# The first block's norm sums: squares made one pair of tiles at a time, GpSimd adds some of them, and TensorE sums half as many tiles

## The reference

```python
def rmsnorm(x, g):
    xf = x.astype(jnp.float32)
    y = xf * lax.rsqrt(jnp.mean(xf * xf, axis=-1, keepdims=True) + EPS)
    return y.astype(x.dtype) * g

for l in range(DEPTH):                                   # DEPTH = 2
    mod = c_act @ w_ada[l] + b_ada[l]                    # shift, scale, gate, twice
    hdn = modulate(rmsnorm(x, norm1_g[l]), shift1, scale1)        # norm 1: 1024 features
    proj = hdn @ w_in[l]
    q = to_heads(rmsnorm(q_lat, q_norm_g[l]) @ w_uq[l], ...)      # q latents: 768 features
    kv = to_heads(rmsnorm(c_kv, kv_norm_g[l]) @ w_ukv[l], ...)    # kv latents: 256 features
    ...                                                  # three kinds of attention, gates, merge
    x = x + gate1[:, None, :] * (merged @ w_out[l])
    hdn = modulate(rmsnorm(x, norm2_g[l]), shift2, scale2)        # norm 2: 1024 features
    ff = jnp.square(jax.nn.relu(hdn @ w_ff1[l])) @ w_ff2[l]
    x = x + gate2[:, None, :] * ff
```

## Time and profile before

| | |
|---|---|
| runs, median (lowest to highest) | 1454.99 us (1454.37 to 1455.53) |
| profiled execution, span from first to last instruction | 1450.2 us |
| around that span, against the median of the runs | 4.8 us (the profiled execution has no time of its own beside its span) |
| TensorE busy | 1393.0 us, 96% |
| VectorE busy | 832.6 us, 57% |
| ScalarE busy | 752.3 us, 52% |
| GpSimd busy | 128.2 us, 9% |
| granted TensorE clock, mean | 0.991 |

### The profile page before, as it was taken

One profiled execution on the slowest core, in us unless ns is written; L12 is line 12 of the kernel. 1 busy time (PEld: TensorE's weight loads), 2 busy tenths in 40 slices (PEclk: granted clock), 3 DMA queues, 4 the chain that ended last, 5 costly groups with the idle time before them and its releaser, 6 DMA issues.

```text
span 1450.2 us, 25075 instructions
## 1 busy us (share of the span) xinstructions
PE 1393.0 (96%) x10568; PEld 1262.0 (87%) x10568; DVE 832.6 (57%) x1256; ACT 752.3 (52%) x1219; POOL 128.2 (9%) x68
## 2 busy tenths in 40 slices
PE   5999999998999998998999999999999999999988
PEld 2988888997999998998999988999998778688978
DVE  3547765556688775468655466444473635428562
ACT  3465565664645534565666546454553564325562
POOL 0000000100000000000000100000003433134321
PEclk8999999999999999999999999999999999999999
DMA  9954566455789994642744558865451222022330
GB/s 355 356 189 159 196 232 206 146 203 181 240 313 351 350 365 154 210 146 87 269 152 140 181 168 287 288 236 172 146 183 59 74 71 88 30 96 88 123 110 30
DMA packets 194723, 269.56 MB, mean 186 GB/s; under 512 B 5037, under 2 KB 174386, under 8 KB 188338
## 3 DMA queue, kind: packets, MB, share of 16 engines
q1 hardware_dynamic: 194610, 267.94, 53.7%
HBM read 266.88 MB, written 1.05 MB: 185 GB/s over the span
## 4 chain that ended last, share of the span: by engine, by line
PE 80%; DVE 10%; ACT 4%; issue 2%; DMA 2%; SPq 1%; DVEq 0%; ACTq 0%
PE first_dense L1654 13%; PE first_dense L1658 12%; PE first_dense L1656 12%; PE first_dense L1012 5%; PE first_dense L1015 5%; PE first_dense L1014 5%; PE first_misc L234 2%; PE first_dense L1821 2%; DVE first_w_lo L555 2%; PE first_s L1654 2%; PE first_s L1658 2%; PE first_s L1656 2%; DMA first_units<-in_w_ada 2%; ACT first_w_hi L549 1%; PE first_o L1658 1%
## 5 line engine op out<-in xcount | busy, mean ns | idle before, releaser
L555 DVE TENSOR_TENSOR first_w_lo<-first_raw,first_w_hi 128x1024 fp32r<-128x1024 f32 (+2 forms) x304 | 363.9, 1208 | 290.0 <-ACT first_w_hi L549 289.0
L549 ACT ACTIVATE first_w_hi<-first_raw 128x1024 fp32r<-128x1024 f32 (+2 forms) x304 | 314.1, 1041 | 253.7 <-PE first_dense L1658 109.0
L1654 PE MATMUL first_dense<-first_h_parts,first_w_hi 128*128 128x256 f32 x1312 | 375.7, 286 | 3.3 <-DVE first_h_parts L2259 3.3
L1658 PE MATMUL first_dense<-first_h_parts,first_w_lo 128*128 128x256 f32 x1312 | 371.8, 283 | 0.0
L1656 PE MATMUL first_dense<-first_h_parts,first_w_hi 128*128 128x256 f32 x1312 | 371.8, 283 | 0.0
L1654 PEld LDWEIGHTS first_dense<-first_h_parts,first_w_hi 128*128 128x128 f32 x1312 | 252.3, 192 | 15.3 <-issue 11.2
L1656 PEld LDWEIGHTS first_dense<-first_h_parts,first_w_hi 128*128 128x128 f32 x1312 | 252.4, 192 | 0.1
L1658 PEld LDWEIGHTS first_dense<-first_h_parts,first_w_lo 128*128 128x128 f32 x1312 | 252.3, 192 | 0.0
L712 POOL TENSOR_TENSOR first_w_lo<-first_raw,first_w_hi 128x1024 fp32r<-128x1024 f32 x41 | 100.5, 2454 | 478.0 <-ACT first_w_hi L705 478.0
L1014 PE MATMUL first_dense<-first_parts,first_w_hi 128*128 128x512 f32 (+1 forms) x384 | 130.8, 341 | 0.0
L1012 PE MATMUL first_dense<-first_h_parts,first_w_hi 128*128 128x512 f32 (+1 forms) x320 | 112.1, 350 | 0.9 <-DVE first_w_lo L712 0.9
(11 more groups left out here) (391 smaller groups left out, 2784.1 us busy)
## 6 DMA issues: line engine op xcount, KB each, us to landing
first_raw<-in_w_in SPq DMA_DIRECT2D x78, 1024.0 KB, 5.0
first_raw<-in_w_ff SPq DMA_DIRECT2D x64, 1024.0 KB, 6.7
first_units<-in_w_ada SPq DMA_DIRECT2D x34, 1024.0 KB, 6.6
first_units<-in_w_mod SPq DMA_DIRECT2D x17, 1024.0 KB, 6.4
first_raw<-in_w_out SPq DMA_DIRECT2D x16, 1024.0 KB, 5.0
first_mb<-in_w_ada SPq DMA_DIRECT2D x10, 1024.0 KB, 8.1
first_mb<-in_w_mod SPq DMA_DIRECT2D x7, 1024.0 KB, 7.2
first_raw<-in_w_uq SPq DMA_DIRECT2D x6, 768.0 KB, 4.2
```

What stands on the lines that cost most here:

```text
L549: act.activation(w_hi[g % SPLIT][:, c], raw[g % CHUNK_RING][:, c], ACT.Copy).then_inc(hi_made, 1)
L555: dve.tensor_tensor(w_lo[g % SPLIT][:, c], raw[g % CHUNK_RING][:, c], w_hi[g % SPLIT][:, c].bitcast(F32), ALU.subtract).then_inc(lo_made, 1)
L1654: pe.matmul(out, still[0](t), moving[0](t), start=start and t == n == 0, stop=False, skip_group_check=True)
L1658: last = pe.matmul(out, still[1](t), moving[0](t), start=False, stop=stop and t == nk - 1, skip_group_check=True)
```

## The change

The squares of x are made pair by pair. In the steps 40 to 43 ScalarE, first thing, waits for the residual of the chunk before and squares its two tiles; in the last three steps of layer 0 it does the same for layer 1, whose last pair comes at that layer's start. GpSimd adds the second pair to the first, and then the third; TensorE sums the tiles 0 and 1 (which hold the sum of six) and then 6 and 7. For the q latents GpSimd adds the pairs of tiles 2, 3 and 4, 5 to the tiles 0, 1, for the kv latents tile 7 to tile 6; TensorE sums two tiles and one. A semaphore `sq_added` counts the additions: five in layer 0, seven in layer 1. Nothing else of the program changes.

```diff
+            def norm_added(norm):
+
+                return {NORM1: 2, NORM_Q: 2, NORM_KV: 3, NORM2: 5}[norm] + (2 if l and norm != NORM1 else 0)
@@ tensor
                 def sum_squares(norm):
 
-                    for t in range(KT):
-                        if t % 2 == 0:
-                            reach(pe, sq_ready, 4 * (norm == NORM2) + t // 2 + 1)
-                        last = pe.matmul(ssq[norm], ones, sq[:, t, :], start=t == 0, stop=t == KT - 1)
+                    reach(pe, sq_added, norm_added(norm))
+                    for t in (0, 1, 6, 7):
+                        if t == 6:
+                            reach(pe, sq_ready, 4 * (norm == NORM2) + 4)
+                        last = pe.matmul(ssq[norm], ones, sq[:, t, :], start=t == 0, stop=t == 7)
                     last.then_inc(ssq_done.sem, 1)
 
                 def latent_squares(norm):
 
-                    lo, hi = (0, 6) if norm == NORM_Q else (6, 8)
-                    for t in range(lo, hi, 2):
-                        wait_evacuated(pe, RING[base + QL + t // 2])
+                    lo, hi = (0, 2) if norm == NORM_Q else (6, 7)
+                    reach(pe, sq_added, norm_added(norm))
@@ scalar
-                def squares(norm):
-                    for t in range(0, KT, 2):
...
+                def square_pair(i):
+                    return act.activation(sq[:, 2 * i:2 * i + 2, :], keep.x[:, 2 * i:2 * i + 2, :], ACT.Square)
@@
                 if l:
-                    squares(NORM1)
+                    reach(act, x_ready, 4)
+                    square_pair(3).then_inc(sq_ready.sem, 1)
                     rstd_start(NORM1, D)
@@
                 for j in range(N_CHUNKS):
+                    if WOUT < j <= FF:
+                        wait_evacuated(act, RING[base + j - 1])
+                        square_pair(j - WOUT - 1).then_inc(sq_ready.sem, 1)
+                    if following and j > FF + 28:
+                        reach(act, following["x_ready"], j - FF - 28)
+                        square_pair(j - FF - 29).then_inc(sq_ready.sem, 1)
                     if j == FF:
-                        squares(NORM2)
                         rstd_start(NORM2, D)
@@ gpsimd
+                def add_squares(to, source):
+                    nonlocal added
+                    if added:
+                        reach(pool, sq_added, added)
+                    added += 1
+                    pool.tensor_tensor(sq[:, to, :], sq[:, to, :], sq[:, source, :], ALU.add).then_inc(sq_added.sem, 1)
+
+                if l:
+                    for i in (1, 2):
+                        reach(pool, sq_ready, i + 1)
+                        add_squares(slice(0, 2), slice(2 * i, 2 * i + 2))
                 for j in range(N_CHUNKS):
+                    if j in (QL + 1, QL + 2):
+                        wait_evacuated(pool, RING[base + j - 1])
+                        wait_evacuated(pool, RING[base + j])
+                        add_squares(slice(0, 2), slice(2 * (j - QL), 2 * (j - QL) + 2))
+                    if j == CKV:
+                        wait_evacuated(pool, RING[base + j])
+                        add_squares(slice(6, 7), slice(7, 8))
+                    if j in (WOUT + 2, WOUT + 3):
+                        reach(pool, sq_ready, 4 + j - WOUT)
+                        add_squares(slice(0, 2), slice(2 * (j - WOUT - 1), 2 * (j - WOUT - 1) + 2))
```

More of the change, by code:

```diff
@@ L201 @@
 ROUND = float(1.5 * 2 ** 23)
-FIRST_COUNTS = dict(sq_ready=8, ssq_done=4, rstd_guess=4, ssq_used=4, full_ready=16, h_hi_made=16, h_ready=16,
+FIRST_COUNTS = dict(sq_ready=8, sq_added=5, ssq_done=4, rstd_guess=4, ssq_used=4, full_ready=16, h_hi_made=16, h_ready=16,
                     lat_scaled=2, lat_hi_made=8, lat_ready=8, rope_swapped=6, rope_done=6,
@@ L1622, in layers, with layer @@
         first_sems = {n: m.sem(n) for n in FIRST_COUNTS}
-        def layer(l, next_x_ready):
+        def layer(l, next_x_ready, following=None):
             base = l * N_CHUNKS
             cols, mod = all_cols[:, l, :], all_mod[:, l, :]
-            sq_ready, ssq_done, rstd_guess, ssq_used, full_ready, h_hi_made, h_ready = (
-                Counted(first_sems[n], FIRST_COUNTS[n] * l) for n in ("sq_ready", "ssq_done", "rstd_guess", "ssq_used", "full_ready", "h_hi_made", "h_ready"))
+            sq_ready, sq_added, ssq_done, rstd_guess, ssq_used, full_ready, h_hi_made, h_ready = (
+                Counted(first_sems[n], FIRST_COUNTS[n] * l) for n in ("sq_ready", "sq_added", "ssq_done", "rstd_guess", "ssq_used", "full_ready", "h_hi_made", "h_ready"))
             lat_scaled, lat_hi_made, lat_ready = (Counted(first_sems[n], FIRST_COUNTS[n] * l) for n in ("lat_scaled", "lat_hi_made", "lat_ready"))
@@ L2073, in gpsimd @@
             def gpsimd(pool):
-                for j in range(N_CHUNKS):
+                added = 0
+                def add_squares(to, source):
[8 more added lines that the diff above has]
+                        add_squares(slice(0, 2), slice(2 * i, 2 * i + 2))
+                for j in range(N_CHUNKS):
+                    if j in (QL + 1, QL + 2):
[8 more added lines that the diff above has]
+                        add_squares(slice(0, 2), slice(2 * (j - WOUT - 1), 2 * (j - WOUT - 1) + 2))
                     if WMB <= j < GA:
@@ L2270, in layers @@
         later = layer(1, x2_ready)
-        first = layer(0, later[-1]["x_ready"].sem)
+        first = layer(0, later[-1]["x_ready"].sem, later[-1])
         stages = [first, later]
```

## The result

| | before | after |
|---|---|---|
| median of the runs (lowest to highest) | 1455.18 us (1454.37 to 1455.53), 4 runs | 1447.58 us (1444.92 to 1448.85), 4 runs |
| ratio to before, 95% interval | | 0.9949 (0.9935 to 0.9964) |
| span of the profiled execution | 1450.2 us | 1447.0 us (its time 1448.85) |
| mean granted clock of it | 0.991 | 0.989 |

A forecast was written before the change was run, and what follows sets the result against it. TensorE, busy 1393.0 of 1450.2 us, was taken as the bound. Norm sums -7.8 and clock +0.5 made -7.3 us, from 1454.99 to 1447.7 us; range 1443.2 to 1451.2.

The forecast's parts named there:

- The tails of the norm sums: At three norms, four TensorE rows instead of sixteen behind the last square: 2.6 us each, 7.8 us gained.
- The early squares: ScalarE's squares of 0.61 us ahead of weight halves, 1.2 us of cover left: costed at nothing, 5.5 us without cover.
- GpSimd's additions: Twelve additions, slowing a VectorE weight subtraction beside one by 0.3 us: taken as 0, far end 3.6 us.
- Rival 4: At VectorE's weight halves, GpSimd's twelve additions hold VectorE still 1.75 us each: 21 us against 7.3, 1468.7 us; 4%.
- The latents: TensorE's latent sums lose 2.3 us a layer but lie beside VectorE's chain: taken as 0, far end 4.5 us.
- Rival 1: The shorter latent sums pay too, by a shorter VectorE chain: another -4.5 us, 1442.7 us; 8%.
- The clock: Behind TensorE's longer pause at layer 0's latents the granted clock falls: 0.5 us lost; 0 more in layer 1 and norms.
- rival 2: Clock falls at the norms and longer at layer 1's latents, taking 7.1 us back: 1454.3 us; all 3%, some 17%.
- a shift ahead of 340 of more than a microsecond either way: Sign of being wrong: before 340 us in the profile, times move by more than a microsecond.
- the shifts forecast for 553, 866 and the end: Stations in the profile after: 553 comes 2 us earlier, 866 about 4.7 earlier, the end 7.3.
- a wait for GpSimd at the norms: Sign of being wrong: the norm sums wait for GpSimd in the profile after.
- slow weight halves in a row with TensorE waiting for them: Sign of being wrong: VectorE's halves of 1.5 us and more in a row, with TensorE waiting for them.

The follow-up runs named there:

- experiments 1: Changed kernel with only its norm part; TensorE sums the latents as in the kernel before, without GpSimd's latent additions: 1445.45 us, ratio 0.9934 to before.
- 6: Full change unaltered and the norms-only kernel, both run again on one chip: 1445.77 us (0.9940 to before) and 1445.33 us (0.9938).
- 7: Norms-only kernel plus matmuls nobody reads in TensorE's pause at the norms, eight rows at norm 1, four at each norm 2: 1445.84 us, 0.9937 to before.
- Experiment 2: Change's latent part only, GpSimd's three latent additions kept, norms as in the kernel before: 1453.94 us, ratio 0.9998 to before.
- experiment 3: Changed kernel with early squares but no GpSimd additions for the norms; TensorE sums all 8 tiles: 1449.82 us, ratio 0.9961 to before.
- Experiments 4: Changed kernel, but GpSimd also adds the last pair of squares and TensorE sums two tiles behind it: 1453.58 us, ratio 0.9989 to before.
- experiment 5: Changed kernel with its additions, but the four squares in a row where the kernel before makes them: 1464.48 us, ratio 1.0064 to before.

## Why the prediction was right, and where not

**The tails of the norm sums: -7.8. Right.** Three times 2.6 were forecast, and 2.58 to 2.60 measured at each, in two profiles of after and in three of experiments 1, 6 and 7. The sub-steps hold too: four early rows, 0.86 of wait, four late ones, no wait for GpSimd. One reading was wrong: the prediction took the pause behind the sum, 1.49 in the earlier trace rows, for that of all three places. At norm 1 of layer 1 it was longer before the change already:

```profile
562.24 0.35 PE L1821 MATMUL first_dense<-first_h_parts,first_w_hi 128*128 128x256 f32 x1 [2.35 <-ACT first_h_parts L1936]
```

It moved up with the rest and stayed at 2.35, so the sum is not touched; but this is the place at which the clock fell, see below.

**The early squares: nothing. Right.** Nothing moves between 200 and 345 us in either profile, and the weight half right behind the third square starts where TensorE lets it:

```profile
348.43 1.06 ACT L549 ACTIVATE first_w_hi<-first_raw 128x1024 fp32r<-128x1024 f32 x1 [1.30 <-PE first_dense L1662]
```

This is the half that stood at 346.04 in the earlier trace rows, later by the 2.4 us by which everything ahead of norm 2 is later. Of its 1.82 us of idle time 1.30 are left behind the square; 1.2 had been forecast.

**GpSimd's additions: nothing. Right, and their length too.** Twelve of 0.73 to 1.81 us (number: duration in ns, lowest, median, highest), against the 1.29 to 2.21 of the earlier trace rows:

```profile
L2085 POOL TENSOR_TENSOR first_sq<-first_sq x12: 730/1716/1814, 96.5 to 858.3; 128x512 f32<-128x512 f32 x10, 128x256 f32<-128x256 f32 x2
```

A weight subtraction beside one takes 1.55 us, as in the earlier trace rows:

```profile
96.52 1.27 POOL L2085 TENSOR_TENSOR first_sq<-first_sq 128x512 f32<-128x512 f32 x1 [95.23 <-ACT first_sq L1998]
...
97.32 1.55 DVE L555 TENSOR_TENSOR first_w_lo<-first_raw,first_w_hi 128x1024 fp32r<-128x1024 f32 x1 [2.56 <-ACT first_w_hi L549]
```

The longest subtraction grew from 1532 to 1752 ns, and the line's busy time from 363.9 to 366.2, 2.3 us in all. It shows as a shift only for a moment, behind the first latents' addition of a layer: VectorE is 0.3 late at 95 and at 620 us of before, in every profile that has these additions and in no other, and back in place by 110 and 640. So its weight is 0.3 to 0.5 us an instruction, not the whole length of an addition. The Trainium skill, GPSIMD Engine Reference, section Key points, names the contention of GpSimd with VectorE's instructions of two SBUF inputs, and gives no amount; the rows agree with the contention. Rival 4 is out.

**The latents: nothing. Right.** Experiment 2 gives 0.9998, and experiments 1 and 6 can't tell the kernel with this part from the one without. Rival 1, -4.5 more, is out. TensorE's lead of 2.3 us a layer comes back as waits: 1.5 us of it in layer 0 (0.96 new, 0.97 where the earlier trace rows have 0.45), 1.4 in layer 1 (4.00 and 0.30 for 1.95 and 0.98); in layer 1 the low clock lasts longer too (672.3 to 679.1), at no cost beyond the +0.2 and -0.3 of the table. The rest I did not trace. After's rows in layer 1:

```profile
672.81 1.27 PE L1788 MATMUL first_o<-first_small,first_area 128*64 128x256 f32 x3 [4.00 <-DVE first_small L2200]
675.23 0.55 PE L1658 MATMUL first_dense<-first_w_hi,first_h_parts 128*128 128x256 f32 x1 [0.30 <-DVE first_w_lo L555]
683.66 0.38 PE L1743 MATMUL first_s<-keep_neg_bf,keep_ident_bf 128*128 128x128 bf16 x4 [0.73 <-issue]
```

**The clock: +0.5 in layer 0. Right in kind, wrong as a fixed term.** The fall came in one profile of after (0.5 us, from 160.5 to 163.9), not in the other, with the same waits before it. Of the six profiles with these additions it came in two (the second of after, experiment 3), and in none of the four without them. The price was right: 0.47 and 0.44. In layer 1 the fall that the earlier trace rows show was not fixed either: in both profiles of the norms alone, with pauses like those of the earlier trace rows, it is missing, and the stretch is 0.5 shorter. I had taken one execution's clock as the kernel's. For the norms I took 0, since the pauses "stay as long as they are or get shorter"; behind norm 1 it fell in the first profiles of after, of the norms alone and of experiment 3, and the stretch behind it then grew by 1.5 us each time, near the 1.65 worked out. That belongs to rival 2, to which I gave 17% for a part of it; in the median of the runs the part was too small to move the forecast. Experiments 4 and 5 show where it would have decided: with 3.59 and 5.00 us of pause it fell at all three norms.

**Not foreseen: 412 to 457.** Between two stations in the feed-forward part 0.8 and 1.3 us went, where TensorE waits for VectorE in the row products (1.2 us before, 0.4 after, no such wait again). In all nine other profiles the stretch is shorter by what this wait is shorter, to 0.1: with the latents alone by 0.5, with the norms alone by 0.6 and 1.3, and in experiment 5, where the norm comes later than before, by 1.1. So it does not follow the change, and the profile of before had the longest such wait of them all. Why it varies is not shown.

**A sign of being wrong that came.** The prediction named "a shift ahead of 340 of more than a microsecond either way" as such a sign, and the shift there was +2.4 us in both profiles of after. Of it 3.9 and 1.9 come in the first 60 us, where the clock stood at 0.50 for other lengths of time than before; the first profile gains 1.5 back at 117, the second loses 0.5 behind the latents. The shift was +1.9 also in the second profile of the norms alone, whose program up to 330 us is that of before, and +0.5 in the first. So all but the 0.5 belongs to the execution and not to the change, and the sign was set too tight: one execution differs from the next by more than a microsecond there. For the same reason the shifts forecast for 553, 866 and the end (2, 4.7 and 7.3 earlier) read 1.0, 1.9 and 3.2 in after and 1.5, 4.5 and 6.0 in its second profile. The other two signs, a wait for GpSimd at the norms and slow weight halves in a row with TensorE waiting for them, did not come.

**The sum.** -7.3 was forecast. The medians differ by 7.6 in the first comparison and by 9.2 in the second, whose ratio of 0.9940 makes 8.7, with an interval from 6.7 to 10.9. The norms alone and the filler differ by 8.8 to 9.6. All these intervals hold 7.8; whether there is another microsecond of gain behind the norms' 7.8, and from what, the runs do not show. That 1447.7 was hit to 0.1 us is partly luck: the 4.8 us that I added to the span were not what lies around it. That is 1.8, and the other 3 were the difference between one quick execution and the median one. The step was still the right one: the terms are differences, and hold for the median execution as for the quick one. But the reading "span plus surroundings" was wrong.

## What to carry to other kernels

A sum that runs behind the last of several producers is worth shortening by moving the producers first, and only then by giving part of it to an idle engine: here the early squares alone gave 2.0 of 2.6 us a place, the additions 0.6 with them, and the additions with late squares made the kernel slower by 0.6%, a good half of it by the clock. Work taken from TensorE in a stretch whose chain of waits has no TensorE piece gave nothing back, however idle the other engine is. And before one profiled execution's clock enters a sum, look at a second execution: the same pause of 2.35 us was followed by a loss of 1.5 us in one and by none in the next.

## What the runs showed of the hardware

- The granted clock is not the same from execution to execution of one kernel on one chip. Between 30 and 45 us it was 0.89 in the profile of before and 0.54 and 0.66 in the two of after, with transfers near 370 GB/s each time, and VectorE's instructions at 110 us came 3.9 and 1.9 us later. In the norms alone of the second batch it was 0.66 too, and 2.0 later. The runs of before spread over 8 us in one batch (1451.03 to 1459.38). A profile of the second run of after, 30 to 45 us:

```profile
30.00:45.00 15.00, 11.36 (x66) 9.57 (x67) 11.04 (x22) 6.83 (x13) 0.00 (x0) 0.66 0.99 374
```

- After a pause of 2.35 us behind a norm the clock was at 0.50 for 3.5 us in some executions and at 1.00 in others. After 3.59 and 5.00 us it was at 0.50 (1.2 of 2.4 GHz) at all three norms, in one profile each.
- A weight subtraction on VectorE (float32, 128x1024) took 1.23 us alone and 1.55 to 1.75 beside a GpSimd addition of 128x512.
- Filling such a pause with matmuls that nobody reads cost nothing, and gained nothing that its runs show.
- GpSimd adds 128x512 in float32 in 1.27 to 1.81 us and 128x256 in 0.73.
